# Weight blocks of the adaLN modulation: from GpSimd accumulation to TensorE matrix-vector products

## The reference

```python
def ada_modulation(c, w, b, n_chunks):
    m = jax.nn.silu(c) @ w + b
    return jnp.split(m[:, None, :], n_chunks, axis=-1)
...
shift, scale, gate = ada_modulation(c, a_ada_w[l], a_ada_b[l], 3)
u = rms_norm(h, a_norm_g[l]) * (1 + scale) + shift
...                                     # attention of layer 0: o
h = h + gate * (o @ a_w_out[l])
kv_shift, kv_scale = ada_modulation(c, kv_ada_w, kv_ada_b, 2)
...
shift, scale, gate = ada_modulation(c, b_ada_w[l], b_ada_b[l], 3)
```

## Time and profile before

| what | us |
| --- | --- |
| median of 3 runs | 1421.94 |
| the profiled execution, first to last instruction (span) | 1417.4 |
| difference between the two | 4.5 |
| TensorE busy | 1201.2 |
| VectorE busy | 1082.1 |
| ScalarE busy | 715.0 |
| GpSimd busy | 437.0 |
| mean of L489, 56 times | 1.859 |
| mean of L487, 54 of its 56 times | 0.944 |
| L762, first to last start (8 units apart by 7) | 143.4 to 740.6 |

### The profile page before, as it was taken

The page is one execution under the profiler, slowest core; times in us unless marked ns, Lnnn a source line. Parts: engine busy times, 40 slices in busy tenths (PEclk is TensorE's granted clock), DMA queues, the critical chain, the costliest instruction groups (busy, mean ns, idle before and its releaser), DMA issues.

```text
span 1417.4 us, 23583 instructions
## 1 busy us (share of the span) xinstructions
PE 1201.2 (85%) x6448; PEld 1018.8 (72%) x6448; DVE 1082.1 (76%) x3159; ACT 715.0 (50%) x2035; POOL 437.0 (31%) x538
## 2 busy tenths in 40 slices
PE   0479898998989889898895799579999999995998
PEld 0368777777777777777775688567888787884786
DVE  5669988889888897988897522896898989987321
ACT  0746555565555545555464200884656666564200
POOL 1235454445454445445342022111021212110122
PEclk9989999999999999999998899779999999998899
DMA  8341221311213122221311434301011110203332
GB/s 306 110 140 40 69 83 34 103 53 56 84 53 96 40 83 68 63 77 39 104 50 50 155 133 142 125 16 60 12 57 31 41 45 25 61 18 100 105 131 93
DMA packets 53227, 111.62 MB, mean 79 GB/s; under 512 B 5904, under 2 KB 19216, under 8 KB 52112
## 3 DMA queue, kind: packets, MB, share of 16 engines
q1 hardware_dynamic: 53136, 110.71, 24.1%
HBM read 93.90 MB, written 16.78 MB: 78 GB/s over the span
## 4 chain that ended last, share of the span: by engine, by line
PE 51%; DVE 30%; issue 12%; ACT 3%; DMA 2%; DVEq 1%; POOL 0%; POOLq 0%; SPq 0%; ACTq 0%
PE ps_p L576 7%; PE ps_p L577 7%; PE ps_p L578 7%; PE ps_s L659 4%; DVE ez L1264 3%; DVE e L1197 3%; DVE qn L1237 2%; PE ps_p L783 2%; PE ps_p L784 2%; PE ps_p L785 2%; PE ps_o L785 2%; PE ps_o L783 2%; PE ps_o L784 2%; PE ps_t L751 2%; PE ps_t L747 2%
## 5 line engine op out<-in xcount | busy, mean ns | idle before, releaser
L576 PE MATMUL ps_p<-w_hi,u_hi 128*128 128x512 f32 x768 | 324.3, 422 | 12.0 <-DVE w_lo L1075 8.5
L578 PE MATMUL ps_p<-w_hi,u_lo 128*128 128x512 f32 x768 | 306.4, 399 | 0.0
L577 PE MATMUL ps_p<-w_lo,u_hi 128*128 128x512 f32 x768 | 306.4, 399 | 0.0
L576 PEld LDWEIGHTS ps_p<-w_hi,u_hi 128*128 128x128 f32 x768 | 148.9, 194 | 35.7 <-DVE w_lo L1075 8.9
L578 PEld LDWEIGHTS ps_p<-w_hi,u_lo 128*128 128x128 f32 x768 | 148.1, 193 | 33.8
L577 PEld LDWEIGHTS ps_p<-w_lo,u_hi 128*128 128x128 f32 x768 | 149.2, 194 | 22.2
L474 POOL TENSOR_TENSOR zs<-stage,ez 128x128 f32<-128x128 f32 (+1 forms) x96 | 56.9, 592 | 336.5 <-DVE ez L1264 336.5
L916 ACT ACTIVATE e<-e,negm 128x256 f32<-128x256 f32 (+7 forms) x128 | 99.3, 776 | 119.5 <-DVE negm L1197 119.3
L659 PE MATMUL ps_s<-kT,qT 128*128 128x384 f32 (+3 forms) x384 | 100.6, 372 | 44.8 <-DVE negm L1197 44.5
L1197 DVE CUSTOM_DVE_ANT_0 e<-ps_s,bias 128x256 f32<-128x256 f32 (+7 forms) x128 | 95.8, 748 | 41.9 <-PE ps_s L659 24.9
L659 PEld LDWEIGHTS ps_s<-kT,qT 128*128 128x128 f32 x384 | 69.1, 201 | 73.4 <-DVE negm L1197 65.5
(11 more groups left out here) (179 smaller groups left out, 3063.0 us busy)
## 6 DMA issues: line engine op xcount, KB each, us to landing
adabuf<-ada_w SPq DMA_DIRECT2D x64, 384.0 KB, 3.2
raw<-w_a SPq DMA_DIRECT2D x80, 256.0 KB, 3.5
raw<-w_b SPq DMA_DIRECT2D x48, 256.0 KB, 3.3
e<-ada_w SPq DMA_DIRECT2D x4, 1024.0 KB, 4.7
stage<-ada_w SPq DMA_DIRECT2D x4, 1024.0 KB, 4.9
e<-x SPq DMA_DIRECT2D x8, 512.0 KB, 3.4
oa_scratch<-ob SPq DMA_DIRECT2D x64, 64.0 KB, 1.6
e<-oa_scratch SPq DMA_DIRECT2D x8, 512.0 KB, 4.5
```

What stands on the lines that cost most here:

```text
L576: pe.matmul(o, u_hi[:, c, t], w_hi[:, c, :], start=(c == 0), stop=False)
L577: pe.matmul(o, u_hi[:, c, t], w_lo[:, c, :], start=False, stop=False)
L578: mm = pe.matmul(o, u_lo[:, c, t], w_hi[:, c, :], start=False, stop=(c == KD - 1))
```

## The change

The scaled blocks, the accumulator and its sum over partitions go. In each of the 64 slots TensorE now takes the loaded block itself as six weight tiles of 128 x 128 and multiplies each by column i of `csil`, the 128 values of silu(c) for that chunk. The results are single columns in the bank of `ps_o` that the slot uses, in columns 256 to 279, four slots to a bank. These products stand behind the second sub-head's scores and ahead of the product with V. VectorE adds the four columns of each bank in slots 6 and 7 (a reduction from PSUM), then bias and the two halves. SyncE's load of a block waits for TensorE's products of two slots before, in place of GpSimd's addition. Where before TensorE waited once per unit for the modulation sum, that wait goes.

```diff
--- before.py
+++ after.py
@@ -134,7 +134,7 @@
         ol = sb("ol", [P, 256])
         ob = sb("ob", [P, 2, 256])
         adabuf = sb("adabuf", [P, 3 * ADAW])
-        ada_acc = adabuf[:, 0:ADAW]
+        ada_sum = sb("ada_sum", [P, 2, ADAW // P])
         prm = sb("prm", [P, N_PAR])
         ident = sb("ident", [P, P])
         identr = sb("identr", [P, P], F32R)
@@ -280,9 +280,8 @@
         b_esnk = sem("b_esnk")
         b_nsink = sem("b_nsink")
         ada_loaded = [sem(f"ada_loaded{k}") for k in range(2)]
-        ada_scaled = sem("ada_scaled")
-        ada_acc_done = sem("ada_acc_done")
         ada_mm = sem("ada_mm")
+        ada_part = sem("ada_part")
 
         block = ctx.enter_context(nc.Block())
 
@@ -341,7 +340,7 @@
                             sp.wait_ge(S.st[k], 16 * ((units - 1) * NT // 2 + 1))
                             sp.dma_start(e0[:, k, :], o_dram[k * P:(k + 1) * P, :]).then_inc(c_o[k], 16)
                     if with_ada and live(0):
-                        at_least(sp, ada_acc_done, 8 * u + i - 1)
+                        at_least(sp, ada_mm, 8 * u + i - 1)
                         sp.dma_start(adabuf[:, ADAW * (1 + i % 2):ADAW * (2 + i % 2)],
                                      ada1_w[u, i, :, :]).then_inc(ada_loaded[i % 2], 16)
                     if live(0) and i >= 2:
@@ -472,21 +471,6 @@
                         st = stage[:, (i - 2) % 4, :]
                         pool.wait_ge(S.zr, n + 1)
                         pool.tensor_tensor(zs[:, (i - 2) % 8, 0:zw], st[:, zc:FW], ez[:, i % 2, 0:zw], ALU.mult).then_inc(S.zg, 1)
-                    if live(0) and is_a:
-
-                        src = adabuf[:, ADAW * (1 + i % 2):ADAW * (2 + i % 2)]
-                        pool.wait_ge(ada_loaded[i % 2], 16 * (4 * u + i // 2 + 1))
-                        at_least(pool, ada_acc_done, 8 * u + i)
-                        if i == 0:
-
-                            at_least(pool, ada_mm, u)
-                            stand_alone(pool, pool_passed)
-                            pool.tensor_scalar(ada_acc, src, csil[:, 0:1], 1.0, ALU.mult, ALU.mult).then_inc(ada_acc_done, 1)
-                        else:
-                            stand_alone(pool, pool_passed)
-                            pool.tensor_scalar(src, src, csil[:, i:i + 1], 1.0, ALU.mult, ALU.mult).then_inc(ada_scaled, 1)
-                            pool.wait_ge(ada_scaled, 7 * u + i)
-                            pool.tensor_tensor(ada_acc, ada_acc, src, ALU.add).then_inc(ada_acc_done, 1)
                 pipeline(pool, 8, units, 6, slot)
 
             def out_sums(n0):
@@ -694,15 +678,22 @@
 
                         pe.wait_ge(S.m, 2 * units * NT)
                         gate_rows(gate)
+                    if is_a and live(0):
+
+                        at_least(pe, S.oadd, n5 - 1 if live(5) else 0)
+                        pe.wait_ge(ada_loaded[i % 2], 16 * (4 * u + i // 2 + 1))
+                        for j in range(ADAW // P):
+                            c0 = 256 + (ADAW // P) * (i // 2) + j
+                            mm = pe.matmul(ps_o[:, i5 % 2, c0:c0 + 1],
+                                           adabuf[:, ADAW * (1 + i % 2) + j * P:ADAW * (1 + i % 2) + (j + 1) * P],
+                                           csil[:, i:i + 1], start=True, stop=True)
+                        mm.then_inc(ada_mm, 1)
                     if live(5):
                         pe.wait_ge(S.phi, n5 + 1)
                         pe.wait_ge(S.plo, n5 + 1)
                         if is_a:
                             pe.wait_ge(S.v, n5 + 1)
                             at_least(pe, S.oadd, n5 - 1)
-                            if i == 2 and live(10):
-
-                                pe.wait_ge(s_mod, 3 + u)
                             o = ps_o[:, i5 % 2, :]
                             for j in range(i5 + 1):
                                 pe.matmul(o[:, 0:256], p_hi[:, j * P:(j + 1) * P], vs[:, j, :], start=(j == 0), stop=False)
@@ -753,15 +744,6 @@
                         mm.then_inc(S.pt, 1)
                     if live(1) and not projected:
                         project(S, is_a, u1, i1, n1, range(late, KD))
-                    if is_a and i == 0 and live(8):
-
-
-                        pe.wait_ge(ada_acc_done, 8 * u)
-                        pe.wait_ge(S.oadd, n5 + 1)
-                        for j in range(ADAW // P):
-                            mm = pe.matmul(ps_o[:, i5 % 2, 500 + j:501 + j], ada_acc[:, j * P:(j + 1) * P], ones[:, :],
-                                           start=True, stop=True)
-                        mm.then_inc(ada_mm, 1)
                 pipeline(pe, 8, units, 6, slot)
 
             def output(n0, u0):
@@ -1285,15 +1267,25 @@
                             dve.wait_ge(S.ol, n5 + 1)
                             at_least(dve, S.st[i5 % 2], 16 * (4 * (u + (i - 5) // 8) + i5 // 2))
                             if is_a:
-                                dve.tensor_tensor(ob[:, i5 % 2, 0:P], ps_o[:, i5 % 2, 0:P], ol[:, 0:P],
-                                                  ALU.add).then_inc(S.oadd, 1)
-                                if i == 1 and live(9):
-
-                                    dve.wait_ge(ada_mm, u)
-                                    c0 = ADA0 // P + (ADAW // P) * (u - 1)
-                                    dve.tensor_tensor(mod[:, bass.ds(c0, ADAW // P)],
-                                                      ps_o[:, (i5 - 1) % 2, 500:500 + ADAW // P],
-                                                      prm[:, bass.ds(c0 + C_ADAB, ADAW // P)], ALU.add).then_inc(s_mod, 1)
+                                last = dve.tensor_tensor(ob[:, i5 % 2, 0:P], ps_o[:, i5 % 2, 0:P], ol[:, 0:P], ALU.add)
+                                if live(0) and i >= 6:
+                                    dve.wait_ge(ada_mm, 8 * u + i + 1)
+                                    last = dve.tensor_reduce(
+                                        ada_sum[:, i % 2, :],
+                                        ps_o[:, i5 % 2, 256:256 + 4 * (ADAW // P)].rearrange("p (c j) -> p j c", j=ADAW // P),
+                                        AX.X, ALU.add)
+                                last.then_inc(S.oadd, 1)
+                                if live(0) and i >= 6:
+                                    dve.wait_ge(S.oadd, n5 + 1)
+                                    c0 = ADA0 // P + (ADAW // P) * u
+                                    if i == 6:
+                                        dve.tensor_tensor(ada_sum[:, 0, :], ada_sum[:, 0, :],
+                                                          prm[:, bass.ds(c0 + C_ADAB, ADAW // P)],
+                                                          ALU.add).then_inc(ada_part, 1)
+                                    else:
+                                        dve.wait_ge(ada_part, u + 1)
+                                        dve.tensor_tensor(mod[:, bass.ds(c0, ADAW // P)], ada_sum[:, 0, :],
+                                                          ada_sum[:, 1, :], ALU.add).then_inc(s_mod, 1)
                                 dve.wait_ge(S.oadd, n5 + 1)
 
                                 at_least(dve, S.var, s - 1)
```

## The result

The changed kernel takes 1495.6 us (1492.2 to 1501.2, 4 runs) against 1422.6 us for the kernel before: a ratio of 1.052, 95% interval 1.050 to 1.054. It is slower, as forecast, but by 73 us and not by 37, and lies 8 us above the range.

What follows compares the result with a forecast made beforehand. TensorE bounds slots 5 to 7 and takes turns with VectorE in slots 1 to 4. Per unit -0.2 - 1.7 + 4.0 + 1.9 + 1.0 = +5.0 us, +37.0 in all: 1459 us, range 1430 to 1488.

Steps and rivals of the forecast that it cites:

- Removed from GpSimd: One scaling and one addition per slot, 2.8 us, 179 us over 64 slots, none on the chain; worth VectorE's relief.
- The 1.25 us in slot 1: At slot 1's end L1250 no longer stalls, so L1272 waits only for ScalarE's input: 1.25 us gained.
- Nothing for slots 5 to 7: No gain from VectorE's relief in slots 5 to 7, where TensorE is not waiting.
- Added to TensorE: Six one-column products per slot behind the second scores, 1.34 us a slot; +4.0 us per unit in slots 5 to 7.
- The load: Block reaches TensorE 1.5 us too late in slot 7; +1.9 us for slots 5 to 7, about 0.5 in slot 2.
- Slot 0: Behind the loop's turn, 1.34 us of products in, 1.34 out; +1.0 us per unit for a clock drop.
- rival A: Clock not regained in slots 1 and 4, slot 0 losing the full 1.7 us: 1481 us, chance 0.20.
- The clock: TensorE's granted clock regained in slots 1 and 4 as waits fill: 0.8 and 1.7 us gained per unit.
- B: Rival: blocks come in time and slot 0 keeps its clock; 2.1 us a unit, 1439 us, chance 0.19.
- C: Rival: faster, VectorE's relief in slots 1 to 4 is the larger; -4.1 us a unit, 1395 us, chance 0.10.
- D: Rival: the pieces cancel within 0.2% (2.8 us) of the kernel before; chance 0.05.
- signs named ahead: Profile after: products 1.3 us per slot, block waits in slots 5 and 6, slots 5 to 7 29.6 us, units 90.3.

Runs made afterwards that it cites:

- none_early_turn: early_turn without TensorE's products (sums are of constants, modulation left out; blocks still loaded): 1374.6 us, ratio 0.967 to the kernel before.
- early_turn: early_load with the one load that slot 0 issues held back until VectorE has begun the masked maximum behind the loop turn: 1447.9 us, ratio 1.018.
- early_load: The changed kernel with each block's load issued a whole slot earlier, ahead of the store it stood behind: 1469.4 us, ratio 1.034.
- no_products: The changed kernel with TensorE's new products left out, blocks still loaded and VectorE adding up constants: 1422.4 us, ratio 1.000.
- early_turn_wide: early_turn with each product against 64 equal columns in place of one: 1436.6 us, ratio 1.011.

## Why the prediction was right and wrong

The direction was right, and the profile's bound too: VectorE's relief doesn't pay for products on TensorE. The runs give each term in turn, here beside what the prediction's sum had over the whole kernel (its unit terms times seven, with unit 0 and the end):

| term | forecast, us | measured, us | from |
| --- | --- | --- | --- |
| GpSimd's relief, with its clock and the old L762 | -48 | -47 | none_early_turn against before |
| products, with their clock | +68 | +73 | early_turn against none_early_turn |
| late blocks | +17 | +26 | after against early_load |
| fetch at the turn held up by a block | 0 | +21 | early_load against early_turn |
| sum | +37 | +73 | |

The forecast's products are 8.0 us a unit behind the waits they fall into, 5.4 us in unit 0, and the 1.0 us a unit for slot 0's clock. The terms add up from the other side as well: without products, taking away both obstacles gave 1422.4 - 1374.6 = 48 us, with products 1495.6 - 1447.9 = 48 us. Each measured term holds for the order in which it was taken.

Point by point. **Removed from GpSimd**: right in size, by luck in part. That the total came out within 1 us is luck, since the parts lie elsewhere. The 1.25 us in slot 1 was taken from one stalled L1250; the stall went (340 ns median now, 475 at most), but TensorE's wait for VectorE's combination stayed, 2.79 us in slot 1 of none_early_turn for 2.57. "Nothing for slots 5 to 7" was wrong by 0.9 us and slot 4 gave twice what was counted. **Added to TensorE**: right. The twelve take 1.26 us in a stream and cost 4.06 us in slots 5 to 7 (26.72 in early_turn less 22.66 in none_early_turn), against 4.0 forecast. **The load**: the mechanism was right and stood where it was put, 1.05 us ahead of the products in slot 5, 0.43 in slot 6 and 0.17 in slot 7, against 1.4, 0.5 and none forecast. The term was short because each wait was costed by its own length alone. The waits themselves come to 18.1 us in the seven units, 2.6 us a unit, close to the 2.4 forecast. But in slots 2 to 4 the clock falls to 0.86 to 0.88 in some units, and with the block in time it doesn't. Together the block's lateness cost 4.9 us a unit, a period of 95.96 in place of 91.07 us ((775.5 - 138.0) / 7, from the row below), twice that. On the mean of six units early_load is 3.0 us shorter in slots 5 to 7, where 1.9 were forecast, and 3.2 us shorter in slots 2 to 4, where 0.5 were; slot 0 is 1.1 us longer.

```profile
...
L1291 DVE TENSOR_TENSOR mod<-ada_sum x8: 165/305/307, 138.0 to 775.5; 128x6 f32 x7, 128x6 f32<-128x6 f32 x1
```

**Slot 0** is the step that failed. "I add 1.0 us for a drop of the clock there" took the turn's hole as it was before. The prediction followed the load only to its reader. It had both facts, that the load follows L1250 and that TensorE falls behind L1250, but didn't ask what else TensorE's lateness moves, nor what else used the DMA queues at the time: VectorE's branch now comes 1.6 us behind L1250's end instead of 0.16, the block of slot 0 is issued 0.5 us ahead of the branch instead of 1.0 us behind it, and VectorE's instruction fetch comes out behind the block. That cost 21 us, and the sum had nothing for it. With the longer hole (3.57 for 1.93 us) and narrow products behind it TensorE then ran at 1.2 GHz for (1 - 0.72) x 2 x 18.32 = 10.3 us, which is 5.1 us of work, against the 1.0 us of the forecast and rival A's 1.7. The unit that the prediction read was also one whose slot 0 kept its clock before; two of six did not. **The clock** in slot 1 came back to 1.00 in all six units and in slot 4 in four of six, as the forecast had it. Rival A, the clock not regained, would have been wrong there and nearer in slot 0, and at 1481 us it too was short. Rivals B, C and D are out: B by the waits, C by the sign, D by the size. (B's working leaves slot 2's 0.5 us of waiting in, though in B the block is in time; without it B would be some 1435 us.)

Of the signs named ahead, the products, the waits' places but for slot 7's 0.17 us, L1250's 0.34 us, the long L1082 (now L1064) and slots 5 to 7 (29.05 us for 29.6) came true. The period, 95.96 us for 90.3, did not, and in the unit shown slot 0 holds 4.1 us of it, slot 1 1.4 us.

## What to carry to other kernels

When an edit makes one engine later against another, look at what the loads will now run beside: here no load was issued sooner against the store it follows, but VectorE's branch fell behind it, so a 384 KB block met the instruction fetch at the loop's end, and a wait of one line gave 21 us back (in early_load; on the changed kernel alone it wasn't tried). Price the work for the engine that is the bound at its full time and look first for another engine with idle time of that length in the same slot: ScalarE did GpSimd's scalings for 0.94 us a slot in a hole, and that kernel is 1.9% faster than the kernel before, while the change, with all of the modulation on TensorE, made it 5.2% slower. And a null result needs its own obstacles checked: leaving the products out gave 0 us where the relief, with the old L762, was worth 47.

## What the runs showed that was not expected

VectorE's instruction fetch at a loop's turn did not overtake a weight block in any turn of these runs. With a block issued ahead of the branch it starts 1.3 to 2.0 us behind the branch in the changed kernel and 2.2 to 2.6 us in early_load; with none ahead, 1.0 us in the kernel before and in early_turn. VectorE goes on 2.2 to 2.4 us after the start of the fetch in all four. That the fetch queues behind the block's packets is read from these times, from the one run that moved the block, and from the turns of no_products; whether it shares their rings or only their engines is open.

Slot 0 takes one of three lengths in early_turn and early_turn_wide: 12.9 to 13.2, 14.4 to 14.6 or 16.1 to 16.3 us, at a mean granted clock of 1.00, 0.88 or 0.79. Products of 64 columns in place of one cost nothing at full clock (slots 5 to 7 take 26.69 us for 26.72) and gave back 11 us in one setting and 21 us in another. What in them keeps the clock up, the columns or the time that the array is busy, wasn't tried.
